# Four slots of split weights moved 80 bytes apart in address phase, product rows aligned, and single-pass constant products at seven norms

## The reference

```python
def first_block(x, ...):                      # two layers
    for l in range(2):
        x = x + hybrid_mixer(rmsnorm(x), w_in[l], ..., w_out[l])   # pooling + attention
        h = rmsnorm(x)
        if l == 0:
            x = x + (silu(h @ wg) * (h @ wu)) @ wd                 # D_FF = 2816
        else:
            x = x + moe_swiglu(h, w_router, wg, wu, wd)            # 8 experts, top 2, D_FF = 3584
    return rmsnorm(x, final_norm)

def second_block(x, c, ...):                  # two layers, each: FFN, mixer of three attentions, FFN
    for layer in range(2):
        mod = silu(c) @ w_ada[layer] + b_ada[layer]
        x = x + 0.5 * g1 * swiglu(modulate(rmsnorm(x), sh1, sc1), w1[0], w3[0], w2[0])
        x = x + g2 * (out_g * rms(attentions(modulate(rmsnorm(x), sh2, sc2) @ w_in)) @ w_out)
        x = x + 0.5 * g3 * swiglu(modulate(rmsnorm(x), sh3, sc3), w1[1], w3[1], w2[1])
    return x
```

## Time and profile before

| | |
|---|---|
| median of three runs | 2462.81 us (2461.85 to 2464.23) |
| span of the profiled execution | 2461.3 us |
| TensorE busy | 2426.1 us, 99% |
| weight loads busy | 2210.0 us, 90% |
| VectorE busy | 2038.9 us, 83% |
| ScalarE busy | 1535.8 us, 62% |
| GpSimd busy | 174.7 us, 7% |
| HBM read | 683.29 MB, 283 GB/s over the span |

### The profile page before, as it was taken

One profiled execution on the slowest core, in us unless ns is written; L12 is line 12 of the kernel. 1 busy time (PEld: TensorE's weight loads), 2 busy tenths in 40 slices (PEclk: granted clock), 3 DMA queues, 4 the chain that ended last, 5 costly groups with the idle time before them and its releaser, 6 DMA issues.

```text
span 2461.3 us, 44012 instructions
## 1 busy us (share of the span) xinstructions
PE 2426.1 (99%) x17074; PEld 2210.0 (90%) x17074; DVE 2038.9 (83%) x2626; ACT 1535.8 (62%) x2090; POOL 174.7 (7%) x244
## 2 busy tenths in 40 slices
PE   9999999999999999999999999999999999999999
PEld 9999998899999998888898899988899899988998
DVE  5688866888988899999998799786898898787665
ACT  5644565777777777878776644557544544567543
POOL 2111021000000000000010111011011011010000
PEclk9999999999999999999999999999999999999999
DMA  7698554999999999999999688443687587432541
GB/s 295 229 366 309 201 185 157 398 365 384 370 382 369 383 378 394 394 390 392 385 391 372 239 319 308 158 148 127 245 319 295 220 316 293 152 129 82 218 181 76
DMA packets 136637, 696.20 MB, mean 283 GB/s; under 512 B 16528, under 2 KB 16656, under 8 KB 87728
## 3 DMA queue, kind: packets, MB, share of 16 engines
q1 hardware_dynamic: 109872, 598.79, 64.5%
q0 software_dynamic: 23424, 88.16, 9.3%
q10 hardware_dynamic: 3136, 6.43, 0.7%
HBM read 683.29 MB, written 13.24 MB: 283 GB/s over the span
## 4 chain that ended last, share of the span: by engine, by line
PE 83%; DVE 7%; ACT 4%; DMA 4%; issue 2%; POOL 0%; SPq 0%; ACTq 0%; DVEq 0%; POOLq 0%
PE ps L2460 16%; PE ps L2056 15%; PE ps L2057 14%; PE ps L2058 14%; PE ps L2627 9%; PE ps L2462 8%; DMA ring<-wstream 4%; DVE w_parts L1745 2%; DVE w_parts L1358 1%; PE ps L2592 1%; PE ps L2085 1%; PE ps L2081 1%; ACT w_parts L1147 1%; DVE a_parts L1752 1%; ACT w_parts L824 1%
## 5 line engine op out<-in xcount | busy, mean ns | idle before, releaser
L2460 PE MATMUL ps<-a_parts,w_parts 128*128 128x512 f32 x1760 | 618.9, 393 | 1.5 <-DVE a_parts L1323 1.3
L2056 PE MATMUL ps<-w_parts 128*112 128x256 f32 x1792 | 520.9, 291 | 8.9 <-DVE w_parts L1745 7.8
L1745 DVE TENSOR_TENSOR w_parts<-ring,w_parts 128x2048 fp32r<-128x2048 f32 x222 | 506.4, 2281 | 0.0
L2058 PE MATMUL ps<-w_parts 128*112 128x256 f32 x1792 | 499.0, 278 | 0.0
L2057 PE MATMUL ps<-w_parts 128*112 128x256 f32 x1792 | 499.0, 278 | 0.0
L2462 PE MATMUL ps<-a_parts,w_parts 128*128 128x256 f32 x1760 | 492.7, 280 | 0.0
L1147 ACT ACTIVATE w_parts<-ring 128x2048 fp32r<-128x2048 f32 x222 | 424.3, 1911 | 18.5 <-DMA ring<-wstream 18.3
L2460 PEld LDWEIGHTS ps<-a_parts,w_parts 128*128 128x128 f32 x1760 | 329.8, 187 | 75.5 <-issue 3.7
L2056 PEld LDWEIGHTS ps<-w_parts 128*112 128x112 f32 x1792 | 313.4, 175 | 45.3 <-issue 38.8
L2462 PEld LDWEIGHTS ps<-a_parts,w_parts 128*128 128x128 f32 x1760 | 332.3, 189 | 0.0
L2057 PEld LDWEIGHTS ps<-w_parts 128*112 128x112 f32 x1792 | 312.9, 175 | 6.5
(11 more groups left out here) (288 smaller groups left out, 4390.1 us busy)
## 6 DMA issues: line engine op xcount, KB each, us to landing
ring<-wstream SPq DMA_DIRECT2D x378, 1024.0 KB, 7.8
ring<-wstream SPq DMA_DIRECT2D x378, 512.0 KB, 5.9
proj<-astream POOLq DMA_DIRECT2D x144, 512.0 KB, 5.6
slot_rows<-branch POOLq DMA_DIRECT2D x7, 448.0 KB, 7.2
slot_out<-slot_rows POOLq DMA_DIRECT2D x1, 3136.0 KB, 14.8
sq<-slot_rows ACTq DMA_DIRECT2D x49, 64.0 KB, 5.2
slot_out<-pT ACTq DMA_DIRECT2D x49, 64.0 KB, 4.8
vtok<-crow POOLq DMA_DIRECT2D x3, 512.0 KB, 3.8
```

Source lines behind the costliest of these rows:

```text
L1745: nc.vector.tensor_tensor(up_lo[:, n % 2, :], ring[:, s, 0:UP], up_hi[:, n % 2, :], ALU.subtract).then_inc(up_used, 1)
L2056: mm(o, stationary[0], moving[0], start=start, stop=False, skip_group_check=True)
L2058: return mm(o, stationary[1], moving[0], start=False, stop=stop, skip_group_check=True)
L2460: mm(ps[:, bank, :], hi, a_parts[:, :, k, :], start=k == 0, stop=k == KB - 1, skip_group_check=True)
```

## The change

There are three edits.

1. Each slot of `w_parts` gets 20 unused elements (80 bytes) behind it. High slot 0, high slot 1, low slot 0 and low slot 1 now start at 128, 208, 288 and 368 modulo 1024. A filler tensor `w_end` makes `w_parts` and filler together exactly 1024 bytes larger than `w_parts` was, so that `ring`, `xT`, `hT`, `a_parts`, `sq` and `proj` move by 1024 bytes and keep their phase.
2. `hid_hi` and `hid_lo` are allocated right behind `proj`. They now start at 178304 and 180352, which is 128 modulo 1024, the phase of `a_parts`. What comes behind them up to `top8` moves by 5120 bytes, the rest by 1024; the phases stay.
3. At the norms n = 2, 5, 6, 7, 8, 9 and 10 the six fp32 products of ones and a constant give way to single-pass products of `hid_lo` (loaded) and `hid_hi` (streamed), each shape three times, into the same bank, still unread. Start columns and widths vary. Norms 0 and 1 keep the six.

```diff
+KEEP_BUSY = {
+    2: [(T, 0, P, s) for s in (0, 4, 8, 16, 32, 64, 128)],
...
+    8: [(T, 0, 64, 0), (T, 0, 32, 0), (T, 0, 96, 0), (P, 0, P, 0), (P, 16, P, 0), (T, 48, 112, 0), (T, 0, 96, 16)],
+    9: [(2 * T, 0, P, s) for s in (0, 4, 16, 64)],
+    10: [(c, 0, P, 0) for c in (192, 288, 320, 384, 448)],
+}
+
+W_PAD = 20
...
-        w_parts = sb("w_parts", [P, 2, 2, TILE], fp32r)
-        w_hi, w_lo = w_parts[:, 0], w_parts[:, 1]
+        w_parts = sb("w_parts", [P, 2, 2, TILE + W_PAD], fp32r)
+        w_hi, w_lo = w_parts[:, 0, :, 0:TILE], w_parts[:, 1, :, 0:TILE]
+        sb("w_end", [P, 2 * P - 4 * W_PAD])
...
         proj = sb("proj", [P, 21, T])
+        hid_hi = sb("hid_hi", [P, 2, T], fp32r)
+        hid_lo = sb("hid_lo", [P, 2, T], fp32r)
         branch = sb("branch", [P, 3 * 4 * (16 + T)])
...
-        hid_hi = sb("hid_hi", [P, 2, T], fp32r)
-        hid_lo = sb("hid_lo", [P, 2, T], fp32r)
...
-                if n in HEADS:
+                if n in KEEP_BUSY:
+                    moving, still = (h.rearrange("p b t -> p (b t)") for h in (hid_hi, hid_lo))
+                    for cols, at, width, w_at in KEEP_BUSY[n]:
+                        for _ in range(3):
+                            mm(ps[0:width, 7, 0:cols], still[:, w_at:w_at + width], moving[:, at:at + cols],
+                               start=True, stop=True)
+                elif n in HEADS:
```

More of the change, by code:

```diff
@@ L84 @@
 NORM_AFTER = {0: 2, 2: 6, 3: 8, 4: 9}
+KEEP_BUSY = {
+    2: [(T, 0, P, s) for s in (0, 4, 8, 16, 32, 64, 128)],
+    5: [(T, o, P, 0) for o in (4, 8, 16, 32, 64, 128, 256)],
+    6: [(T, 4, P, 4), (T, 8, P, 8), (T, 16, P, 16), (T, 2, P, 0), (T, 64, P, 64), (T, 12, P, 4), (T, 24, P, 0)],
+    7: [(T, 0, 112, s) for s in (0, 4, 8, 16, 32, 64, 128)],
+    8: [(T, 0, 64, 0), (T, 0, 32, 0), (T, 0, 96, 0), (P, 0, P, 0), (P, 16, P, 0), (T, 48, 112, 0), (T, 0, 96, 16)],
[3 more added lines that the diff above has]
+W_PAD = 20
 SPLITS = [STARTS[i] - (STREAM[MOE_STAGE] if i > MOE_STAGE else 0) for i in range(len(STREAM) + 1)]
```

## The result

The changed kernel takes 2468.12 us (median of 8 runs) against 2461.84 us for the kernel before on the same chip: a ratio of 1.0026, 95% interval 1.0016 to 1.0036. It is slower by a quarter of a per cent, 6.3 us. The forecast was 2452.8 us.

What follows compares the result with a forecast made beforehand. TensorE's start-to-start distances were taken as the bound. Projection and down gave -10 us, all other terms 0: span 2461.3 to 2451.3, plus 1.5 for the median, 2452.8 us; range 2426 to 2484 us.

Steps and rivals of the forecast that it cites:

- What bounds the kernel: Whole kernel: the end is set by the distance from one TensorE product's start to the next, not by busy time.
- Constant products at 0: Seven norms: the new single-pass products finish while the real product waits for data, so cost 0; bound 0.03 us late.
- The row I named as a witness: At each norm, the next real product was to start 2.7 to 2.9 us behind the first constant one.
- Projection and down, -10.0 us: Projections and feed-forward down: 3328 of 4992 products leave phase with their loads, 120 to 117 ns each; bounds -35, +17 us.
- Feed-forward up at 0: 1760 feed-forward up pairs: distance stays 230 + 116 ns, loads being done early; 0, bounds -11 and +7 us.
- Expert up at 0: Expert up, 3360 products that count: 113 and 118 ns about equally frequent, mix may shift either way; 0, bounds 8 us each way.
- the expert chunks leaving 113 altogether: Sign in the expert up chunks that the forecast is wrong; it expected still a mix of 113 and 118 ns.
- Rival "slower", 2484: Streaming from shifted slots costs time in expert up, projection and down: together +21 us, 2484 us; chance of slower 0.30.
- its first half: Expert up: chunks at 113 ns fall to 118 because rows stream from shifted slots, 8 us.
- Its second half: Projection and down: distance goes to 125 ns in half of the cases, 12.5 us.
- Range, 2426 to 2484 us: Whole kernel's time: bounds said to leave out the far half of each outer rival.
- a rule of the Trainium skill: TensorE weight loads: cited for the rival that phases change nothing measurable, 2462.8 us give or take 5; chance 0.23.

Runs made afterwards that it cites:

- lo_parts_only: Kernel before, with only the low halves of feed-forward down parts and projection tiles 160 bytes further inside their slots: 2455.39 us, ratio 0.9974.
- slots_only: Kernel before, with only the four weight slots set 80 bytes apart, hidden rows keeping their phase: 2468.67 us, ratio 1.0026.
- the sweep: Kernel before, with different shifts of down parts, projection tiles and expert tokens in each stage, in one profile: 2465.1 us, a single execution.

## Why the prediction was wrong

By its own steps:

- **What bounds the kernel:** right. What was found to move, moved in the distance between TensorE's starts at a full clock. The distances, with start and scatter, account for 2.7 of the 4.6 us between the spans; see the sum below.
- **Constant products at 0:** right. 1.0002 alone; 3.07 us from the last sum to the real product in both kernels. The row I named as a witness was a poor one: measured from the first constant product it went from 2.85 to 3.04 us, outside the 2.7 to 2.9 forecast, though nothing was late.
- **Projection and down, -10.0 us:** right in sum (-3.9 and -5.9, together -9.8), in part by luck. I had 3 ns for two thirds of the products; measured is 1.7 and 2.2 ns in the mean of all. The reason was only half right. I counted the products that leave the phase between rows and load, and held the hidden rows' move for a part of it. What counts, in every version tried, is the distance between the high and the low half, whichever phase the streamed rows have: with all slots in one phase, down takes 120 ns at either phase of the hidden rows, and in lo_parts_only, where every high part is still in phase with the rows of the projection, that takes 118. And the stall is not "in the load": down had 187 ns loads at 120 ns before, and has 188 ns loads at 118 ns now. The load's duration, on which I built, shows the phase and not the price.
- **Feed-forward up at 0, "the load is in any case done long before":** the first step that failed, +7.9 us. The bound on that side (350 ns a pair, +7 us) was a little short: 352. I took a pair's distance for something fixed by its own operands. It is one of several spacings (pairs of about 347, 351, 354 and 356 ns), and which one a chunk gets depends on its own slots and on the blocks ahead of it.
- **Expert up at 0, "the mix may shift either way":** the second, +7.9 us in distances, of which 3.6 us show in the stage. It went to the bound that I had named, all at 118, but I had mis-sized it: I took 113 and 118 for equally frequent and priced 8 us for the five experts that count, where only 58 of 223 chunks were at 113. The estimate treated 113 and 118 as a toss that can fall either way. It falls one way: the kernels in which slots, tokens and halves share one phase in the expert stage have 58 to 75 chunks at 113, the slots 80 bytes apart leave 26, and low slots 160 bytes on, tokens 8 columns on, or the changed kernel leave none. The prediction had named this, the expert chunks leaving 113 altogether, as a sign that it was wrong.
- **Rival "slower", 2484:** its first half, the experts, is what came. Its second half, projection and down at 125, didn't: no version has either above 120 ns in the mean.
- **Range, 2426 to 2484 us:** I gave it as leaving out the far half of each outer rival. The upper end is the slower rival's own value, so that rule doesn't give it. The measured 2468.12 us lies inside, on the side that I had not forecast.

The sum with the measured terms: -9.8 (projection, down) + 7.9 (up) + 3.6 (the expert stage, its down products in it) + 1.0 (start and scatter) = +2.7 us, against +4.6 in the spans and +6.3 in the medians. The 1.9 us between the terms and the spans lie in the feed-forward and mixer stages, outside the distances that I averaged. The stages' lengths hold them, the terms don't, and their cause stays open. The runs' own difference of 1.7 us more lies within what single executions scatter.

The prediction weighed a rule of the Trainium skill: "TensorE: Matmul & The Clock Gate", Part 2 (step-by-step), says that the array has two independent read ports and that loading the next tile's weights takes nothing from the running product. The runs here do not bear it out as a rule on time. Moving `hid_hi` and `hid_lo` by 416 bytes cost 9.4 us with the same instructions in the same order; whether the reads of the two ports meet somewhere, no run here can show.

What stays open is the mechanism: why a block holds a spacing, and why 80, 160 or 32 bytes choose it. The runs show that it happens within TensorE's own sequence (one short product more changes it, a busy or idle VectorE doesn't). They show that it follows addresses and the blocks before. Moves by whole kilobytes leave it alone, 512 bytes between the slots do too, and 416 bytes between rows and slots don't. Beneath that they show nothing.

## What to carry to other kernels

When TensorE is the bound and its products are a few per cent apart from one another in neighbouring blocks of the same shape, look at start-to-start distances block by block, not at a stage's mean or at durations: here the spacing was a state that a whole block kept. Change the address phase of one kind of product at a time, and read the blocks behind it as well, because a gain in one can be handed back by the next. A padding that applies to a whole buffer reaches every use of it; here the uses wanted opposite things, and offsets by use gave 6 us where the padding of all (slots_only) lost 6.6.

## What the runs showed that I had not expected

- Address phase within SBUF alone is worth -0.26% to +0.39% of this kernel: 2455.4 to 2471.7 us with the same products.
- The 512-column product goes from 231 to 236 ns when the hidden rows, which it doesn't read, are moved by 416 bytes.
- Products of 256 columns with 112 loaded ones run at 113 ns in a quarter of the chunks with tokens and weights in phase; tokens 4 bytes on (expert 7 of the sweep) end it, and all of that expert's chunks are at 117 to 118.
- Effects of address shifts don't add: slots alone +0.26%, hidden rows alone +0.39%, both together with the constant products +0.26%.
